# Expert choice by all groups at once, and token weights in three pieces, in a hybrid mLSTM / sparse-attention / MoE block

## What is computed

```
scores = sigmoid(h @ w_router)                    # 512 x 16
sel = scores + b_router
group_score = sum of the two largest sel in each of 4 groups of 4 experts
best_group = argmax(group_score)
idx = top-2 of sel within best_group              # the first index wins a tie
w = scores[idx] / sum(scores[idx])
y = sum over experts e of w_e * (silu(h @ Wg[e]) * (h @ Wu[e])) @ Wd[e]
```

## Time and profile before

| | us |
|---|---|
| median of 3 executions | 778.35 |
| lowest and highest | 776.97, 778.81 |
| the profiled execution: its time | 774.83 |
| the profiled execution: span from first to last instruction | 773.0 |
| PE busy in the span | 733.4 (95%) |
| DVE busy | 588.6 (76%) |
| ACT busy | 430.0 (56%) |

### The profile page before, as it was taken

How to read it: one execution, slowest core, us unless ns; L and a number is a source line. 1 busy time by engine, 2 the same in 40 slices (tenths; PEclk the granted TensorE clock), 3 DMA queues, 4 the chain that set the end, 5 groups by cost and what they waited for, 6 DMA issues and landing times.

```text
span 773.0 us, 10896 instructions
## 1 busy us (share of the span) xinstructions
PE 733.4 (95%) x4006; PEld 597.7 (77%) x4006; DVE 588.6 (76%) x818; ACT 430.0 (56%) x513; POOL 96.3 (12%) x132
## 2 busy tenths in 40 slices
PE   3899999999999999999999989999999999999995
PEld 3777999987877776878888757888887888888872
DVE  6967999797763545424666789888989899889888
ACT  5652334256445455651230336787786877887755
POOL 5010000000110000000000136311121111122002
PEclk9899999999999999999999999999999999999998
DMA  9665313420273111261359939999999999999163
GB/s 247 184 208 184 110 56 109 164 70 1 89 296 110 55 56 55 59 215 56 109 127 392 336 121 363 405 393 396 403 392 371 387 398 397 395 397 389 41 235 156
DMA packets 105394, 172.50 MB, mean 223 GB/s; under 512 B 21216, under 2 KB 42032, under 8 KB 105164
## 3 DMA queue, kind: packets, MB, share of 16 engines
q1 hardware_dynamic: 94928, 152.84, 55.7%
q0 software_dynamic: 4896, 12.95, 4.3%
q10 hardware_dynamic: 5532, 6.20, 2.4%
HBM read 161.61 MB, written 21.10 MB: 236 GB/s over the span
## 4 chain that ended last, share of the span: by engine, by line
PE 86%; DVE 7%; ACT 3%; issue 1%; ACTq 1%; POOL 1%; DVEq 0%; POOLq 0%
PE low L1160 17%; PE low L1161 17%; PE low L1162 17%; PE wide L1160 7%; PE wide L1162 7%; PE wide L1161 7%; PE wide L1568 2%; DVE m_lo L2023 1%; PE low L1445 1%; PE low L1405 1%; PE wide L1376 1%; ACTq L746 1%; PE low L1575 1%; PE wide L1383 1%; PE wide L1581 1%
## 5 line engine op out<-in xcount | busy, mean ns | idle before, releaser
L2023 DVE TENSOR_TENSOR m_lo<-m_raw,m_hi 128x2048 fp32r<-128x2048 f32 x95 | 215.0, 2290 | 28.0 <-ACT m_hi L1014 27.2
L1014 ACT ACTIVATE m_hi<-m_raw 128x2048 fp32r<-128x2048 f32 x95 | 179.6, 1918 | 24.4 <-PE low L1162 23.9
L1160 PE MATMUL low<-m_hi,xe_hi 128*128 128x512 f32 x256 | 102.8, 401 | 2.4 <-DVE m_lo L2023 1.9
L1162 PE MATMUL low<-m_hi,xe_lo 128*128 128x512 f32 x256 | 100.0, 391 | 0.0
L1161 PE MATMUL low<-m_lo,xe_hi 128*128 128x512 f32 x256 | 99.7, 389 | 0.0
L1160 PE MATMUL low<-hT_hi,w_hi 128*128 128x512 f32 (+1 forms) x240 | 94.7, 395 | 3.7 <-DVE hT_lo L1754 2.5
L1718 DVE TENSOR_TENSOR w_lo<-raw,w_hi 128x2048 fp32r<-128x2048 f32 x28 | 64.1, 2290 | 39.1 <-ACT w_hi L741 38.9
L1161 PE MATMUL low<-hT_lo,w_hi 128*128 128x512 f32 (+1 forms) x240 | 92.4, 385 | 0.0
L1162 PE MATMUL low<-hT_hi,w_lo 128*128 128x512 f32 (+1 forms) x240 | 91.9, 383 | 0.0
L741 ACT ACTIVATE w_hi<-raw 128x2048 fp32r<-128x2048 f32 x28 | 53.5, 1911 | 16.6 <-PE wide L1162 8.3
L1160 PEld LDWEIGHTS low<-m_hi,xe_hi 128*128 128x128 f32 x256 | 48.0, 188 | 15.4 <-DVE m_lo L2023 5.0
(11 more groups left out here) (423 smaller groups left out, 1408.5 us busy)
## 6 DMA issues: line engine op xcount, KB each, us to landing
m_raw<-in_w_gate SPq DMA_DIRECT2D x32, 1024.0 KB, 8.3
m_raw<-in_w_up SPq DMA_DIRECT2D x32, 1024.0 KB, 7.9
m_raw<-in_w_down SPq DMA_DIRECT2D x31, 1024.0 KB, 8.9
raw<-in_w_in SPq DMA_DIRECT2D x19, 1024.0 KB, 6.1
raw<-in_w_out SPq DMA_DIRECT2D x4, 1024.0 KB, 5.0
y<-y_dram SPq DMA_DIRECT2D x8, 512.0 KB, 6.7
table_dram<-table_row ACTq DMA_DIRECT2D x1, 2624.0 KB
strips<-table_dram SPq DMA_DIRECT2D x8, 264.0 KB, 4.0
```

The costliest lines, as they stand in the source:

```text
L1014: nc.scalar.activation(m_hi[n % MS][:, :], (m_spare if is_last(n, j) else m_raw[slot])[:, :], ACT.Copy).then_inc(q["m_hi_ready"], 1)
L1160: nc.tensor.matmul(outp, lh, rh, start=first, stop=False)
L1162: return nc.tensor.matmul(outp, ll, rh, start=False, stop=last)
L2023: v.tensor_tensor(m_lo[n % MS][:, :], (m_spare if is_last(n, j) else m_raw[n % MR])[:, :], m_hi[n % MS][:, :].bitcast(F32), ALU.subtract). ...
```

## The change

The four instructions of pair sums and the three of masking go. `best_of_group` finds the first maximum within every group of four at once, all five steps over 64 elements (the two maxima of each group are written into single columns of the old `pairs` tile, 16 groups apart by 6 elements). It is called for the best, one step masks it, and it is called for the second best. The group score is the sum of the two maxima; five steps over 16 elements find the best group, and two products with it give `one1` and `one2`.

The 13 steps of the token weights are split: four after iteration 1 of `j`, five after iteration 3, and four (with `e_rank`) after the last one; DVE's loops are now 0 to 1, 2 to 3 and 4 to 6.

```diff
@@ -2068,29 +2068,29 @@
             step(v.tensor_tensor(full(sel), full(scores), over_t(brout[:, :]), ALU.add))
 
             by4 = lambda t: t[:, :, :].rearrange("p i (g x) -> p (i g) x", g=GROUPS)
-            pair = pairs[:, :, :]
-            step(v.tensor_tensor(pair[:, :, 0:3], by4(sel)[:, :, 0:3], by4(sel)[:, :, 1:4], ALU.add))
-            step(v.tensor_tensor(pair[:, :, 3:5], by4(sel)[:, :, 0:2], by4(sel)[:, :, 2:4], ALU.add))
-            step(v.tensor_tensor(pair[:, :, 5:6], by4(sel)[:, :, 0:1], by4(sel)[:, :, 3:4], ALU.add))
-            step(v.tensor_reduce(grp.rearrange("p i g -> p (i g)"), pair, AX.X, ALU.max))
-
-            def first_max(dst, src, order, tmp, n):
-
-                step(v.tensor_reduce(gm, src, AX.X, ALU.max))
-                step(v.tensor_tensor(tmp, src, gm.to_broadcast([P, TT, n]), ALU.is_equal))
-                step(v.tensor_tensor(tmp, tmp, order, ALU.mult))
-                step(v.tensor_reduce(gm, tmp, AX.X, ALU.max))
-                step(v.tensor_tensor(dst, tmp, gm.to_broadcast([P, TT, n]), ALU.is_equal))
-
-            first_max(grp, grp, order4, grp2, GROUPS)
-
-            step(v.tensor_scalar(grp2, grp, -1.0, 1e30, ALU.add, ALU.mult))
             each = lambda t: t.rearrange("p i (g o) -> p (i g) o", o=1).to_broadcast([P, TT * GROUPS, EG])
-            step(v.tensor_tensor(by4(pick), by4(sel), each(grp), ALU.mult))
-            step(v.tensor_tensor(by4(pick), by4(pick), each(grp2), ALU.add))
-            first_max(full(one1), full(pick), order16, full(t0), NE)
-            step(v.scalar_tensor_tensor(out=full(pick), in0=full(one1), scalar=-1e30, in1=full(pick), op0=ALU.mult, op1=ALU.add))
-            first_max(full(one2), full(pick), order16, full(t0), NE)
+            best1, best2, gmax = [pairs[:, :, i:i + 1] for i in range(3)]
+            in4 = lambda t: t.to_broadcast([P, TT * GROUPS, EG])
+
+            def best_of_group(dst, src, best):
+
+                step(v.tensor_reduce(best.rearrange("p x o -> p (x o)"), by4(src), AX.X, ALU.max))
+                step(v.tensor_tensor(by4(t0), by4(src), in4(best), ALU.is_equal))
+                step(v.tensor_tensor(full(t0), full(t0), order16, ALU.mult))
+                step(v.tensor_reduce(gmax.rearrange("p x o -> p (x o)"), by4(t0), AX.X, ALU.max))
+                step(v.tensor_tensor(by4(dst), by4(t0), in4(gmax), ALU.is_equal))
+
+            best_of_group(t1, sel, best1)
+            step(v.scalar_tensor_tensor(out=full(pick), in0=full(t1), scalar=-1e30, in1=full(sel), op0=ALU.mult, op1=ALU.add))
+            best_of_group(t2, pick, best2)
+            step(v.tensor_tensor(grp.rearrange("p i (g o) -> p (i g) o", o=1), best1, best2, ALU.add))
+            step(v.tensor_reduce(gm, grp, AX.X, ALU.max))
+            step(v.tensor_tensor(grp, grp, gm.to_broadcast([P, TT, GROUPS]), ALU.is_equal))
+            step(v.tensor_tensor(grp, grp, order4, ALU.mult))
+            step(v.tensor_reduce(gm, grp, AX.X, ALU.max))
+            step(v.tensor_tensor(grp, grp, gm.to_broadcast([P, TT, GROUPS]), ALU.is_equal))
+            step(v.tensor_tensor(by4(one1), by4(t1), each(grp), ALU.mult))
+            step(v.tensor_tensor(by4(one2), by4(t2), each(grp), ALU.mult))
             v.tensor_tensor(chosen[:, :, :], full(one1), full(one2), ALU.add).then_inc(q["chosen_ready"], 1)
 
             def xe_lo_out(e):
@@ -2183,26 +2183,30 @@
                 m_split_lo(n + 4, j)
                 m_split_lo(n + 5, j)
 
-            with dve.Fori(0, 3) as j:
+            def two_experts(j):
+
                 expert_dve(j, 0)
                 expert_dve(j, 1)
-            step(v.tensor_copy(e_rank[:, :].rearrange("p (i o) -> p i o", o=1), t3[:, :, NE - 1:NE]))
+
+            as3 = lambda t: t.rearrange("p (i o) -> p i o", o=1)
+            with dve.Fori(0, 2) as j:
+                two_experts(j)
             for k, one in enumerate((one1, one2)):
                 step(v.tensor_tensor(full(t0), full(scores), full(one), ALU.mult))
                 step(v.tensor_reduce(weight[:, k, :], full(t0), AX.X, ALU.add))
-            step(v.tensor_tensor(gm, weight[:, 0, :].rearrange("p (i o) -> p i o", o=1), weight[:, 1, :].rearrange("p (i o) -> p i o", o=1), ALU.add))
+            with dve.Fori(2, 4) as j:
+                two_experts(j)
+            step(v.tensor_tensor(gm, as3(weight[:, 0, :]), as3(weight[:, 1, :]), ALU.add))
             step(v.tensor_scalar(gm, gm, ALPHA, None, ALU.mult))
             step(v.reciprocal(gm, gm))
             for k in range(2):
-                w1 = weight[:, k, :].rearrange("p (i o) -> p i o", o=1)
-                step(v.tensor_tensor(w1, w1, gm, ALU.mult))
-            as3 = lambda t: t.rearrange("p (i o) -> p i o", o=1)
+                step(v.tensor_tensor(as3(weight[:, k, :]), as3(weight[:, k, :]), gm, ALU.mult))
+            with dve.Fori(4, NE // 2 - 1) as j:
+                two_experts(j)
+            step(v.tensor_copy(as3(e_rank[:, :]), t3[:, :, NE - 1:NE]))
             step(v.tensor_tensor(as3(e_weight[:, :]), as3(weight[:, 0, :]), one1[:, :, NE - 1:NE], ALU.mult))
             step(v.tensor_tensor(gm, as3(weight[:, 1, :]), one2[:, :, NE - 1:NE], ALU.mult))
             step(v.tensor_tensor(as3(e_weight[:, :]), as3(e_weight[:, :]), gm, ALU.add))
-            with dve.Fori(3, NE // 2 - 1) as j:
-                expert_dve(j, 0)
-                expert_dve(j, 1)
 
             j = NE // 2 - 1
             hd_lo_out(NE - 2)
```

## The result

The changed kernel takes 773.17 us (median of 7 executions, 770.95 to 773.66), against 778.35 for the kernel before in 7 executions beside them: ratio 0.9939, 95% interval 0.9923 to 0.9955. That is 5.2 us less; forecast were 2.6, and 775.7 us with a range from 773.7. The direction was right, the time lies 0.5 us outside the range.

What follows compares the result with a forecast made beforehand. PE was taken to bound the kernel, with both parts of the change in work it waits for. The choice's 1.0 us and the token weights' 1.6 made 2.6, taken from the median 778.35: 775.7 us, range 773.7 to 778.2.

Steps and rivals of the forecast that it cites:

- What bounds the kernel: PE, busy 95% of the span; after 440 us its waits for `chosen` (1.0 us) and one `m_lo` (1.9) touch the change.
- The choice: DVE's choice of experts: 19 steps instead of 23, 4.60 us instead of 5.61, no stride surcharge; gain 1.0 us.
- everything moves by 1.0: From `chosen` to the first expert: counts, lists, gather, turn and `xe_lo` form a chain, all 1.0 us earlier.
- The token weights: DVE's 13 steps among the experts, split in three: PE's hole of 2.08 us becomes 0.49, gain 1.6 us.
- The spare 0.97 us: Where DVE's iterations meet it waits 0.97 us for ACT, so a piece costs its length less 0.97.
- the 0.19 for a loop's entry: DVE's last step before a loop takes 0.39 us instead of 0.20, so entering a loop costs 0.19.
- the free last piece: Four token-weight steps after iteration 6, 0.82 us with no loop behind them, covered by the 0.97: cost nothing.
- rival 3: A second DVE loop entry costs 0.4 to 0.5 us more per place: weights gain half, 776.6 us; 0.23 together with rival 2.
- the sum: Gains 1.0 + 1.6 = 2.6 us, profiled span 773.0 to 770.4, applied to the median: 778.35 to 775.7; chance 0.49.
- Rival 1: PE keeps its clock at 2.4 GHz ahead of the first expert, about 0.5 us more: gain 3.1, 775.2 us; chance 0.20.
- Rivals 2: PE's unread matmuls before `chosen` end 1 us later, so only the weights gain: 1.6, 776.7 us; 0.23 together with rival 3.
- rival 4: Instruction fetch between DVE's loops, 2.9 us more in both places: 3.2 slower, 781.6 us; decides from 1.3 a place; chance 0.08.

Runs made afterwards that it cites:

- the weights alone: The kernel before with the token weights in three pieces and the old choice of experts; ratio 0.9973 (0.9960 to 0.9986).
- four steps earlier: The changed kernel with four small memset steps of a dead tile on DVE before its wait for `h_loaded`; one execution taken, no time or ratio given.
- the second profile of before: Profile of the kernel before, run again with no edit; ratio 1.0003 (0.9989 to 1.0017), span 777.8 us.
- the filled hole: The kernel before with PE's loop split at iteration 3 and eight unread matmuls put there; ratios 0.9975 and 0.9967, its control without the matmuls 0.9979 and 0.9963.

## Why the prediction was right or wrong

**What bounds the kernel: right.** The two waits of PE that were read from the profile were the two that the change removed.

**The choice: right in its steps, short by a third in its effect.** 19 steps in 4.63 us (4.60 forecast), no surcharge for strides, the gain wholly on the path, `chosen` ready just as the unread matmuls end (in the kernel before PE goes on 0.28 us after `chosen` starts; 447.96 + 0.28 = 448.24, and they end at 448.26). Mis-sized is the sentence that "everything moves by 1.0": it moves by 1.34 (17.57 to 16.23), since DVE resumes 0.35 us sooner behind PE's counts, which no step of the prediction had and no run explains.

**The token weights: right.** 2.08 was to become 0.49; it is 0.54 to 0.55 in the profile of after, and the experts' column falls from 280.3 to between 278.4 and 278.8: 1.5 to 1.9 against 1.6. The spare 0.97 us, the 0.19 for a loop's entry and the free last piece hold. In the weights alone, and with four steps earlier, the second entry showed 0.59 and 0.58 of idle time instead of 0.22: rival 3 at one of its two places, in two profiles, neither of them of the changed kernel itself.

**The step that failed is the sum**: "It was 3.5 us under the median, so I apply the difference to the median". Its base was a median of three executions, 778.35, which lies 1.2 us above the mean of the 123 later ones. And it assumes that the steps counted in one kind execution are the whole gain in a usual one. They are not: the steps make 1.34 + 1.6 = 2.9 us, the means are 4.4 +- 0.3 apart. So the forecast of 775.7 was 2.5 us too high by 1.2 of base, 0.3 of the choice's effect and 1.5 that no counted step has, less 0.4 because the first seven executions of after have their median above the mean of all 19.

**Where the 1.5 might be.** They go with the clock. Across the executions, with one slope for all kernels, 0.001 of mean clock goes with 0.56 us; at equal clock before and after differ by 3.0 +- 0.2 us, the sum of the steps. The mean clock is 0.9887 before and 0.9912 after; 61 of 123 executions have 0.988 or less, against 2 of 19. That is a correlation, not a cause: read by stretches, the profiles have their low clock in four places, and only two of them are near the change. All have some 3.4 or 6.8 us of it in the first 60 us, the longer one in nine profiles, which reach L1544 1.0 us later in the mean; all have some 3.4 us ahead of the first expert (6.9 in the second profile of before, and in the changed kernel with six unread matmuls); two have 3.4 us behind the hole; and all have 4 to 8 us in the last 20. The longer one of the first place stands in six of the nine profiles with the old choice and in three of the eleven with the new one, though nothing that was changed runs there, so part of the difference may be chance.

For the hole among the experts the prediction weighed only its length; the second profile of before shows a second price, 1.6 us, when the clock falls behind it. Of the seven profiles that have PE's 1.9 us wait two show that, of the thirteen others none. 1.6 us in two of seven would be 0.46 in the mean, a third of the 1.5, but the filled hole, built to show it, does not. The longer low clock ahead of the first expert is in one of nine profiles with the old choice and in one of eleven with the new, so it explains nothing. The rest is open.

The Trainium skill (TensorE: Matmul & The Clock Gate, Part 1) says that the gate's phase varies from run to run. The profiles fit that, with the same kernel once keeping its clock behind the hole and once not; they do not show the phase itself.

The first comparison also overstated the gain: its seven executions of before had a mean of 778.0, the 123 others 777.2. 5.2 us were 4.4. A forecast of 2.6 with a range of 4.5 us would still have missed the centre by 1.8.

**Rival 1: near in its number, wrong in its mechanism.** It had 3.1 us from a clock that stays up ahead of the first expert. The profiled span fell by 2.9, but the clock fell there all the same, and the 16 unread matmuls take 5.50 us against 5.51. The changed kernel's busy times from 452 to 454 us (columns as above, granted clock 0.50) and PE's timeline:

```profile
452.00:454.00 2.00, 2.00 (x6) 1.52 (x6) 1.76 (x8) 0.00 (x0) 1.39 (x2) 0.50 0.41 113
```

```profile
451.19 5.50 PE L1581 MATMUL wide<-m_hi 128*128 128x512 f32 x16
```

**Rivals 2, 3 and 4: wrong.** The unread matmuls do not hold the choice up. In the changed kernel's profiles both entries have 0.22 or 0.23 us of idle time, as the one entry of the kernel before has, so nothing of the size of a fetch (1.3 us a place for rival 4 to decide) stops DVE there. The rule of the Trainium skill that rival 4 cites (Runtime: NRT & Kernel Launch, Instruction fetch mechanics) finds no case on DVE here.

## What to carry to other kernels

Where many small steps stand in one engine's stream beside a saturated one, cut them to the idle time that the stream has at each seam, and place them there: here 0.97 us a seam, and a piece of 0.7 costs nothing. Count a hole of TensorE as its length, and look besides whether the clock falls behind it. Before building on one profile or a median of three, take several of the same kernel: two profiled executions of before differed by 4.8 us here, more than the change is worth, and the median of three was 1.2 us off.

## What was not expected of the hardware

After a TensorE wait of 1.9 us the granted clock fell to 0.50 behind it (591.9 to 595.3 us in one) in two of seven profiles, and with a wait of 1.2 us in the one profile taken it did not. Splitting a TensorE hardware loop in two, with no change of work, took 2.0 us off the mean (775.22 against 777.19) and about 1.4 off the tail (32.5 against 33.8 in the mean of their profiles). Small DVE `memset` steps of 4 columns follow each other in 0.125 us where two-operand ones take 0.20.
